# Two transfers through a DRAM row in place of products with a diagonal, in three norms of a hybrid decoder trunk

## The reference

```
def rmsnorm(x, g):
    inv = lax.rsqrt(jnp.mean(xf * xf, axis=-1, keepdims=True) + RMS_EPS)
    return (xf * inv) * g

for i in range(DEPTH):                       # DEPTH = 2
    h = h + mix(rmsnorm(h, mix_norm_g[i]))
    # conv_glu_ffn: u = xn @ w_up; u = conv3(u) + conv_b
    #               (silu(gate) * up) @ w_down, D_FF = 2816
    h = h + conv_glu_ffn(rmsnorm(h, ffn_norm_g[i]), ...)
    gate = sigmoid(rmsnorm(h, ple_norm_g[i]) @ w_ple_gate[i])
    h = h + gate * (p[i] @ w_ple_proj[i])
return rmsnorm(h, final_norm_g)
```

## Time and profile before

| | |
|---|---|
| median of three runs | 1112.18 us (1111.61 to 1112.74) |
| span of the profiled execution | 1110.7 us |
| TensorE busy | 1093.1 us (98%), 5164 products |
| VectorE busy | 732.4 us (66%) |
| ScalarE busy | 537.4 us (48%) |
| GpSimd busy | 19.6 us (2%) |
| moved by DMA | 106.31 MB, mean 96 GB/s |
| chain that ended last | TensorE 92%, VectorE 4%, ScalarE 3% |

### The profile page before, as it was taken

One profiled execution on the slowest core, in us unless ns is written; L12 is line 12 of the kernel. 1 busy time (PEld: TensorE's weight loads), 2 busy tenths in 40 slices (PEclk: granted clock), 3 DMA queues, 4 the chain that ended last, 5 costly groups with the idle time before them and its releaser, 6 DMA issues.

```text
span 1110.7 us, 14486 instructions
## 1 busy us (share of the span) xinstructions
PE 1093.1 (98%) x5164; PEld 911.0 (82%) x5164; DVE 732.4 (66%) x1136; ACT 537.4 (48%) x799; POOL 19.6 (2%) x62
## 2 busy tenths in 40 slices
PE   9999999999999999999999999999999999999994
PEld 8878888888888888888888888888888888888884
DVE  6568888575775377744776878777437763476836
ACT  6458878454643144421445676544214442244645
POOL 0000000020000000000000000000000000000012
PEclk9999999999999999999999999999999999999997
DMA  8112121222233222332234222232322233222302
GB/s 325 64 58 74 42 76 57 73 101 110 83 107 114 76 95 94 98 116 84 97 98 133 95 76 76 88 102 94 114 76 94 95 103 118 75 101 95 136 36 76
DMA packets 30625, 106.31 MB, mean 96 GB/s; under 512 B 3312, under 2 KB 3312, under 8 KB 30576
## 3 DMA queue, kind: packets, MB, share of 16 engines
q1 hardware_dynamic: 30288, 105.13, 28.1%
q10 hardware_dynamic: 288, 0.53, 0.1%
HBM read 103.55 MB, written 2.10 MB: 95 GB/s over the span
## 4 chain that ended last, share of the span: by engine, by line
PE 92%; DVE 4%; ACT 3%; issue 1%; POOL 0%; DVEq 0%; ACTq 0%; POOLq 0%
PE bank L1238 29%; PE bank L1240 29%; PE bank L1239 29%; PE bank L1334 1%; PE bank L1258 1%; DVE h_tok L1183 1%; ACT probs L485 1%; DVE w_lo L804 1%; DVE c L1189 1%; PE bank L1347 1%; DVE c L1181 0%; PE bank L1299 0%; PE bank L1529 0%; PE bank L1613 0%; PE bank L1526 0%
## 5 line engine op out<-in xcount | busy, mean ns | idle before, releaser
L1238 PE MATMUL bank<-x_hi,w_hi 128*128 128x512 f32 x896 | 350.4, 391 | 0.0
L1240 PE MATMUL bank<-x_hi,w_lo 128*128 128x512 f32 x896 | 348.8, 389 | 0.0
L1239 PE MATMUL bank<-x_lo,w_hi 128*128 128x512 f32 x896 | 348.6, 389 | 0.0
L804 DVE TENSOR_TENSOR w_lo<-w_raw,w_hi 128x1024 fp32r<-128x1024 f32 (+1 forms) x189 | 226.0, 1197 | 52.7 <-ACT w_hi L383 52.6
L383 ACT ACTIVATE w_hi<-w_raw 128x1024 fp32r<-128x1024 f32 (+1 forms) x189 | 193.8, 1031 | 109.8 <-PE bank L1240 109.3
L1240 PEld LDWEIGHTS bank<-x_hi,w_lo 128*128 128x128 f32 x896 | 168.2, 188 | 35.3
L1238 PEld LDWEIGHTS bank<-x_hi,w_hi 128*128 128x128 f32 x896 | 168.2, 188 | 34.7 <-issue 0.4
L1239 PEld LDWEIGHTS bank<-x_lo,w_hi 128*128 128x128 f32 x896 | 168.2, 188 | 34.6
L1238 PE MATMUL bank<-g_hi,w_hi 128*128 128x512 f32 x352 | 136.9, 389 | 0.0
L1239 PE MATMUL bank<-g_lo,w_hi 128*128 128x512 f32 x352 | 136.9, 389 | 0.0
L1240 PE MATMUL bank<-g_hi,w_lo 128*128 128x512 f32 x352 | 136.9, 389 | 0.0
(11 more groups left out here) (205 smaller groups left out, 1211.0 us busy)
## 6 DMA issues: line engine op xcount, KB each, us to landing
w_raw<-in_weights SPq DMA_DIRECT2D x189, 512.0 KB, 3.5
gain_and_h<-in_xT SPq DMA_DIRECT2D x7, 256.0 KB, 6.1
out<-emb SPq DMA_DIRECT2D x3, 512.0 KB, 3.1
p_raw<-in_pT SPq DMA_DIRECT2D x1, 1024.0 KB, 10.3
w_raw<-in_weights SPq DMA_DIRECT2D x2, 256.0 KB, 3.6
gain_b<-in_final_gain SPq DMA_DIRECT2D x1, 512.0 KB, 4.2
gain_and_h<-in_gain_and_x ACTq DMA_DIRECT2D x1, 260.0 KB, 3.4
params<-in_columns SPq DMA_DIRECT2D x1, 256.0 KB, 8.1
```

The lines of the kernel that those rows point to most:

```text
L804: dve.tensor_tensor(w_lo[s][:, 0:w], w_raw[s][:, 0:w], w_hi[s][:, 0:w].bitcast(F32), ALU.subtract).then_inc(lo_done, 1)
L1238: pe.matmul(dst, w1, m1, start=start and i == 0, stop=False)
L1239: pe.matmul(dst, w1, m0, start=False, stop=False)
L1240: last = pe.matmul(dst, w0, m1, start=False, stop=stop and i == len(parts) - 1)
```

## The change

Three norms (`NORM_FFN0`, `NORM_PLE0`, `NORM_FFN1`) no longer use diagonal, products and copy. ScalarE writes `icol` (128x4 floats) with a transfer to a row of 512 floats in DRAM (`row_out`), waits for its landing, and reads the row into all 128 partitions of `inv` with a second transfer (`row_in`). VectorE waits for that landing (`row_landed`) where it waited for ScalarE's copy. In the first block the last four embedding copies of ScalarE are cut into two and two, and the second transfer stands between.

```diff
@@ hybrid_trunk
+        row_written, row_landed = sem("row_written"), sem("row_landed")
-        spread_of = {NORM_MIX0: 1, NORM_FFN0: 2, NORM_PLE0: 3, NORM_FFN1: 4}
+        row_of = {NORM_FFN0: 0, NORM_PLE0: 1, NORM_FFN1: 2}
@@ scalar
-            def inverse(norm):
-                act.wait_ge(spread_done, spread_of[norm])
-                act.activation(inv[:, :], bank[7 if norm else 0][:, :], ACT.Copy, scale=float(D_MODEL)).then_inc(inv_done, 1)
+            def row_out(norm):
+                act.wait_ge(icol_done, norm + 1)
+                act.dma_start(inv_rows[row_of[norm]].rearrange("(t p) -> p t", p=P), icol,
+                              allow_slow_non_contiguous=True).then_inc(row_written, 16)
+
+            def row_in(norm):
+                r = row_of[norm]
+                act.wait_ge(row_written, 16 * (r + 1))
+                act.dma_start(inv[:, :], inv_rows[r:r + 1, :].broadcast_to((P, SEQ))).then_inc(row_landed, 16)
@@ scalar, first block
             rms_of(NORM_FFN0)
+            row_out(NORM_FFN0)
             split_hi(PHASES["emb0"][0] + 1 + LOOK)
-            emb_copy(0, 1, PHASES["emb0"][0] + 1)
-            inverse(NORM_FFN0)
+            emb_copy(0, 1, PHASES["emb0"][0] + 1, range(0, 2))
+            row_in(NORM_FFN0)
+            emb_copy(0, 1, PHASES["emb0"][0] + 1, range(2, 4))
@@ scalar, second block
                     rms_of(NORM_FFN1)
+                    row_out(NORM_FFN1)
                     split_hi(PHASES["emb1b"][0] + 1 + LOOK)
-                    inverse(NORM_FFN1)
+                    row_in(NORM_FFN1)
@@ scalar, gate of layer 0
                 rms_of(norm)
+                row_out(norm)
                 split_hi(PHASES[name][0] + LOOK + 1)
                 split_hi(PHASES[name][0] + LOOK + 2)
-                inverse(norm)
+                row_in(norm)
@@ vector, inverse(norm)
-                if norm in spread_of:
-                    spread(icol, parts_done, 2 * spread_of[norm] - 2).then_inc(diag_done, 1)
+                if norm == NORM_MIX0:
+                    spread(icol, parts_done, 0).then_inc(diag_done, 1)
@@ vector, at each of the three places
-            dve.wait_ge(inv_done, spread_of[NORM_FFN0])
+            dve.wait_ge(row_landed, 16 * (row_of[NORM_FFN0] + 1))
@@ tensor
-            def norm_spread(norm):
-                pe.wait_ge(diag_done, spread_of[norm])
-                spread(bank[7]).then_inc(spread_done, 1)
...
-            norm_spread(NORM_FFN0)
...
-                            if first and u == 1 and layer:
-                                weights, moving, ready = parts[KT // 2]
-                                def ready_and_spread():
-                                    norm_spread(norm)
-                                    ready()
-                                parts[KT // 2] = (weights, moving, ready_and_spread)
...
-                    if m == 1:
-                        norm_spread(norm)
@@ kernel
+    inv_rows = nc.dram_tensor("inv_rows", (N_ROWS, SEQ), F32, kind="Internal").ap()
```

More of the change, by code:

```diff
@@ L45 @@
 BAND = P + EDGE
+N_ROWS = 3
 def plan():
@@ L93, in result_of, with hybrid_trunk @@
     return RESULTS_BEFORE[name] + u + 1
-def hybrid_trunk(nc, gain_and_x0, xT, pT, weights, final_gain, columns, out):
+def hybrid_trunk(nc, gain_and_x0, xT, pT, weights, final_gain, columns, out, inv_rows):
     with ExitStack() as ctx:
@@ L387, in rms_of, with first_inverse @@
                 act.activation(rms_col, bank[7][:, 0:TT], ACT.Sqrt, bias=eps[:, 0:1]).then_inc(rms_done, 1)
-            def inverse(norm):
-                act.wait_ge(spread_done, spread_of[norm])
-                act.activation(inv[:, :], bank[7 if norm else 0][:, :], ACT.Copy, scale=float(D_MODEL)).then_inc(inv_done, 1)
+            def first_inverse():
+                act.wait_ge(spread_done, 1)
+                act.activation(inv[:, :], bank[0][:, :], ACT.Copy, scale=float(D_MODEL)).then_inc(inv_done, 1)
+            def row_out(norm):
[6 more added lines that the diff above has]
+                act.dma_start(inv[:, :], inv_rows[r:r + 1, :].broadcast_to((P, SEQ))).then_inc(row_landed, 16)
             act.dma_start(gain_and_h[:, 0:KT + SEQ], gain_and_x0[:, :]).then_inc(x_in[0], 16)
@@ L436, in _ @@
                 act.activation(pT_hi[:, j, :], p_raw[:, j, :], ACT.Copy).then_inc(pT_hi_done, 1)
-            inverse(NORM_MIX0)
+            first_inverse()
             split_hi(8)
@@ L1090, in _ @@
                     split_lo(PHASES["emb1b"][0] + 1 + LOOK)
-                    dve.wait_ge(inv_done, spread_of[NORM_FFN1])
+                    dve.wait_ge(row_landed, 16 * (row_of[NORM_FFN1] + 1))
                 dve.memset(u32[:, :, 0:PAD], 0.0).then_inc(pad_zero, 1)
@@ L1144, in _ @@
                 split_lo(PHASES[name][0] + LOOK + 2)
-                dve.wait_ge(inv_done, spread_of[norm])
+                dve.wait_ge(row_landed, 16 * (row_of[norm] + 1))
                 def next_input(m):
@@ L1725 @@
     result = nc.dram_tensor("out", (1, SEQ, D_MODEL), F32, kind="ExternalOutput").ap()
-    hybrid_trunk(nc, *args, result)
+    inv_rows = nc.dram_tensor("inv_rows", (N_ROWS, SEQ), F32, kind="Internal").ap()
+    hybrid_trunk(nc, *args, result, inv_rows)
     r = run_bass_kernel_spmd(nc, [arrays], core_ids=[0])
```

## The result

The changed kernel takes 1136.78 us (median of 4 runs, 1135.89 to 1137.41), the kernel before 1112.46 us (4 runs): ratio 1.0221, 95% interval 1.0206 to 1.0235. It is **24.3 us slower**. The forecast was 1113.3 us, with a range from 1111.2 to 1117.0.

The account below looks back on a forecast made before the run. TensorE, 98% busy, bounds the kernel: -1.38 us for six products plus a 2.5 us stall in the second block (w + r = 6.4) nets +1.1 us, applied to the 1112.18 median: 1113.3 us, range 1111.2 to 1117.0.

Parts of the forecast that it names:

- What bounds the kernel: Whole kernel: TensorE, busy 98% of the span; a product removed is time gained, a wait reaching TensorE is time lost.
- the price of a product: TensorE: 0.23 us each by the starts, 0.46 us a spread; three spreads removed save 1.38 us.
- rival D: TensorE: the six products are worth their busy time, 0.39 us each, 2.3 us with no stall, 1109.9 us; chance 0.02.
- w: Write of 512 single floats to DRAM, from issue to landing: 3.0 us taken, between 1.9 and 7.2.
- Rival B: Store from icol, second block: write goes float by float, slower from w = 4.1; at w = 5, 1115.3 us; chance 0.23.
- rival A: Both transfers quick: w + r under 4.5, stall under 0.6 us, 1111.1 us, no change; chance 0.10.
- r: Read of the row (256 KB) into all partitions, from issue to landing: 3.4 us taken, between 2.9 and 4.2.
- The path behind the row: Second block: serial chain from row to unit 3's low half of weights, 0.57 us slack left; stall paid once.
- S = w + r - 3.89: TensorE's stall at unit 3 of the second block, forecast at 2.5 us for w + r = 6.4.
- Gate and first block: No stall at layer 0's gate for w + r under 9.2, nor in the first block, where it may exceed 10 us.
- rival C: TensorE's clock falls after a stall, products cost double: 1.5 to 3 us more, 1116 us; chance 0.07.
- Edits called free: ScalarE loses three copies, gains six DMA issues, moves embedding copies; idle time there, so no cost by themselves.

Follow-up runs that it names:

- Two quick rows: Against the kernel before: transfers only in first block and gate, 16-byte pieces, VectorE orders the row once; second block unchanged: 1110.92 us beside 1111.99, ratio 0.9990.
- the quarter: Against the change: only 128 of the 512 floats written, side by side; second transfer reads the final gain, norm factor left out: 1127.26 us in one execution.
- the second block alone: Against the kernel before: transfers only in the second feed-forward block, first block and gate keep diagonal and products: 1123.81 us, ratio 1.0104.
- the filled run: Against the change: 20 spare TensorE products before unit 2 of the first block, 44 before unit 3 of the second: 1132.38 us, 4.4 us faster.

## Why the prediction was wrong

**What bounds the kernel, and the price of a product: right.** Two quick rows gained 1.07 us for four products, 0.92 by the step of 0.23 us. By their busy time (rival D) it would have been 1.6. But the interval of that run (0.9981 to 0.9999) allows 0.1 to 2.1 us, so the time alone doesn't decide; what speaks for 0.23 are the starts, and the 20 and 44 spare products, which cost 4.1 and 9.4 us net of the spread where 0.39 each would be 7.3 and 16.7.

**w, the failed step.** The time of the write was priced by what its pieces occupy, and that was the wrong kind of cost. I took 3.0 us and called 7.2 the upper end, from 32 pieces to an engine at 165 ns each. Measured: 8.6, 9.5 and 11.1. That bound counted what a packet occupies of an engine. It assumed that pieces in flight don't wait for one another, which nothing in the trace of before could show, since no store there has pieces as small as one float. The 3.0 itself holds for the same 512 floats spread out (2.9), so the number of pieces, for which I made room, was not the danger. Rival B had the right place and the right operation, and was given 0.23 and the wrong mechanism (70 ns a piece); the time lies in how close the pieces fall. Of the sentences of the Trainium skill quoted with it (DMA: Bandwidth & Descriptors, "Specifications" and "Rules for kernel authors"), the one on pieces under 512 B being read, modified and written may be why crowded writes wait for one another, but no run here shows the reading. The other, one descriptor per element, agrees with the packets counted (one for each float), but doesn't decide: 512 elements apart land in 2.9 us. The fixed 2.0 us of the Trainium skill (same page, "Anatomy of one DMA") is a fit for transfers issued by GpSimd, and these are ScalarE's; it is 0.9 us under the spread pieces and 7.5 under the change. The sum of 4.6 by that formula is also just above rival A's limit of 4.5, so it didn't quite belong there.

**r: mis-sized.** I took 3.4 us, upper end 4.2. In the change it was 5.4 to 7.6, and 4.0 to 5.3 with the floats 512 bytes apart, where nothing was held up; so 0.6 to 1.9 us of the error are not the slow write's. The 4.2 came from a load whose overlap with others I hadn't looked at. Why this read takes longer than a load of as many bytes no run separates. In the second block w was 6.5 us over my figure (9.5 for 3.0) and r 2.0 (5.4 for 3.4): together the 8.5 us between the stall forecast, 2.5, and the 11.0 that the rule gives for the measured landings.

**The path behind the row: right.** S = w + r - 3.89 gives 14.9 - 3.89 = 11.0 for the second block; TensorE waited 10.65, at unit 3, once. With the floats 512 bytes apart (1.8 us for the write there, 4.0 for the read) it gives 1.9, and the wait was 1.5. It is some 0.4 us high over the whole of that range: with the floats 8 bytes apart it gives 4.9 for 4.5, with the quarter 8.1 for 7.7, with the second block alone 9.9 for 9.5.

**Gate and first block: the slack was right, the verdict not.** "No stall for w + r under 9.2" at the gate; it was 14.7, which makes 5.5 by that rule and was 4.3, in two waits. Only the second was for a low half; the first (1.83 us) was for a bank, since the results that free the banks wait for the row too, a path I hadn't priced. "There w + r may be over 10 us" in the first block; it was 18.7. I had not reckoned it for more than the upper end.

**Clock (rival C): it happened,** at all three places, for 2.7, 1.7 and 1.8 us by the rows, and the filled run shows it to be a cost of its own at two of them. The price I gave (1.5 to 3 us for one place) was of the right size. But B and C were priced one at a time; they came together, since the slow write made the stall.

**Edits called free** on ScalarE and VectorE show in none of the waits.

## What to carry to other kernels

Before a transfer is put on a path of dependence, look at where its pieces fall in DRAM: here many single floats side by side landed in 8 to 11 us, the same floats in 16-byte pieces or 16 bytes apart in 3, and other transfers were held up beside the slow one. Work out the slack of each place against the sum of both landings, take the transfer where the slack covers it and leave the products where it doesn't. A wait that stops TensorE for some microseconds (2.7 were enough in one run) can have a second bill, the clock, which spare products can save.

## What the runs showed of the hardware

- 128 single floats side by side took as long (8.3 us) as 512 (9.5), and 512 spread out a third of it (2.9). The landing follows how many writes fall close together, from 4 in 64 bytes upward.
- One store of 2 KB held up a 512 KB load on another queue, which needed 13.1 us instead of 4.2; a weight load in the second block needed 11.3 where 3.5 is the median.
- The granted clock fell at waits of TensorE of 4.0, 5.0 and 10.65 us, and at the gate after 1.83 and 2.44 us (0.80 in the stretch from 648 to 651, 0.64 in the next). The length of the wait alone doesn't tell: it fell after a single one of 2.73 us (pieces of 16 bytes, second block) and stayed at 1.00 after one of 2.89 (floats 16 bytes apart, the same place). The fall can come after TensorE has gone on: at 707.25 it did, and the clock was at 1.00 until 708.
- A float32 reciprocal on VectorE took 3.35 us for 512 columns.
